# An mLSTM branch's output product as four pairs of seven block products, and an attention branch that adds to it

## The reference

```python
um  = h_m * silu(za);   y_m = um @ w_out_mlstm     # 1024x1024 @ 1024x1024
ua  = o_a * silu(zb);   y_a = ua @ w_out_attn      # 1024x512  @ 512x1024
merged = sigmoid(ga) * y_m + sigmoid(gb) * y_a
x = x + gate * (merged @ w_out)                    # 1024x1024 @ 1024x1024
return rms_norm(x, g_final)
```

## Time and profile before

| | |
|---|---|
| median of 3 runs | 1370.96 us (1369.63 to 1371.36) |
| the profiled execution | 1371.11 us |
| its span, first to last instruction | 1369.3 us |
| outside the span | 1.8 us |
| PE / DVE / ACT / POOL busy | 98% / 62% / 42% / 34% |

### The profile page before, as it was taken

One profiled execution on the slowest core, in us unless ns is written; L12 is line 12 of the kernel. 1 busy time (PEld: TensorE's weight loads), 2 busy tenths in 40 slices (PEclk: granted clock), 3 DMA queues, 4 the chain that ended last, 5 costly groups with the idle time before them and its releaser, 6 DMA issues.

```text
span 1369.3 us, 17469 instructions
## 1 busy us (share of the span) xinstructions
PE 1345.7 (98%) x6453; PEld 1126.9 (82%) x6453; DVE 855.3 (62%) x1472; ACT 580.1 (42%) x1016; POOL 463.0 (34%) x298
## 2 busy tenths in 40 slices
PE   8999999999999999999999999999999999999998
PEld 6888888888888888888898788889878887888886
DVE  7988766573745444535368757866875766434586
ACT  7663353343444344332545446354545534111122
POOL 0096555554545555543002200210120022222551
PEclk9999999999999999999999999999999999999999
DMA  8522323323234343337231841553172165453543
GB/s 316 196 82 95 132 99 123 123 93 115 101 123 139 123 143 134 139 112 228 73 83 48 231 93 32 161 148 94 48 227 67 33 241 205 128 187 140 173 138 108
DMA packets 65454, 180.52 MB, mean 132 GB/s; under 512 B 22001, under 2 KB 22129, under 8 KB 63318
## 3 DMA queue, kind: packets, MB, share of 16 engines
q1 hardware_dynamic: 61082, 166.64, 36.9%
q10 hardware_dynamic: 3168, 8.70, 1.9%
q0 software_dynamic: 1120, 4.06, 1.0%
HBM read 132.49 MB, written 46.89 MB: 131 GB/s over the span
## 4 chain that ended last, share of the span: by engine, by line
PE 87%; DVE 6%; ACT 3%; DMA 2%; issue 1%; SPq 0%; POOL 0%; ACTq 0%; DVEq 0%
PE banks L592 23%; PE banks L594 23%; PE banks L593 23%; PE banks L1265 4%; PE banks L1390 2%; PE banks L1400 2%; PE banks L1350 2%; PE banks L1356 2%; DMA wraw<-in_w_all 1%; PE banks L1339 1%; PE banks L1348 1%; PE banks L1409 1%; PE banks L584 1%; PE banks L556 1%; PE banks L1378 1%
## 5 line engine op out<-in xcount | busy, mean ns | idle before, releaser
L1248 POOL TENSOR_TENSOR wlo<-wraw,whi 128x1024 fp32r<-128x1024 f32 x28 | 72.1, 2575 | 436.5 <-ACT whi L1468 411.1
L718 POOL TENSOR_TENSOR wlo<-w_sum,whi 128x512 fp32r<-128x512 f32 x112 | 165.2, 1477 | 137.4 <-ACT whi L843 137.4
L592 PE MATMUL banks<-t_hi,whi 128*128 128x512 f32 x448 | 174.3, 389 | 0.0
L593 PE MATMUL banks<-t_lo,whi 128*128 128x512 f32 x448 | 174.3, 389 | 0.0
L594 PE MATMUL banks<-t_hi,wlo 128*128 128x512 f32 x448 | 174.3, 389 | 0.0
L989 DVE TENSOR_TENSOR c_sum<-c_sum,banks 128x512 f32<-128x512 f32 x196 | 134.4, 686 | 44.7 <-PE banks L594 30.6
L592 PE MATMUL banks<-h_hi,whi 128*128 128x512 f32 x416 | 162.0, 389 | 0.0
L594 PE MATMUL banks<-h_hi,wlo 128*128 128x512 f32 x416 | 161.9, 389 | 0.0
L593 PE MATMUL banks<-h_lo,whi 128*128 128x512 f32 x416 | 161.8, 389 | 0.0
L843 ACT ACTIVATE whi<-w_sum 128x512 fp32r<-128x512 f32 x112 | 70.5, 630 | 165.5 <-PE banks L594 100.7
L592 PE MATMUL banks<-whi,h_hi 128*128 128x512 f32 x256 | 100.2, 391 | 1.4 <-POOL wlo L1248 1.4
(11 more groups left out here) (374 smaller groups left out, 2904.8 us busy)
## 6 DMA issues: line engine op xcount, KB each, us to landing
wraw<-in_w_all SPq DMA_DIRECT2D x72, 512.0 KB, 4.3
raw<-in_w_all SPq DMA_DIRECT2D x28, 512.0 KB, 4.4
queries_keys<-fin SPq DMA_DIRECT2D x12, 1024.0 KB, 4.0
qa<-queries_keys SPq DMA_DIRECT2D x12, 768.0 KB, 13.7
s_wada<-in_w_ada_cols SPq DMA_DIRECT2D x16, 512.0 KB, 8.2
attn_values<-fin SPq DMA_DIRECT2D x6, 1024.0 KB, 4.0
tn<-attn_values SPq DMA_DIRECT2D x12, 512.0 KB, 10.1
sig_c<-merge_gates SPq DMA_DIRECT2D x6, 1024.0 KB, 6.4
```

Of the source, the lines that this page charges most:

```text
L592: t_.matmul(out, w_hi, x_hi, start=first, stop=False)
L593: t_.matmul(out, w_hi, x_lo, start=False, stop=False)
L718: nc.gpsimd.tensor_tensor(wlo4[:, o % 4, :], source(r, j), whi4[:, o % 4, :].bitcast(F32), subtract).then_inc(s_split, 1)
L1248: nc.gpsimd.tensor_tensor(to, wraw[:, q % 2, :], hi.bitcast(F32), ALU.subtract).then_inc(w_split, 1)
```

## The change

The mLSTM branch's product is made as `blocks` makes its products: four pairs of tiles (`BRANCH_PAIRS`), each of seven products of 12 matmuls, joined in SBUF (`umo`) and multiplied there by the first gate. The attention branch follows for all eight tiles; `merge_tile` now multiplies its half tile by the second gate and adds it to `umo`. Loads, splits, buffers and banks are put in a new order for it. `finish` is unchanged but for names and where it waits.

```diff
 def turn_stats(i):                         # mix, SP queue
+    if i == HEADS - 1:
+        gather_branch()     # um_d -> um_raw tiles 0-3; xc -> um_raw tiles 6, 7 (512 KB each)
-    for q in range(2):
+    for q in range(2) if i < HEADS - 1 else ():
         sp.wait_ge(um_done, i * 2 + q + 1)
         sp.dma_start(um_d[i, q], xc[:, q, :]).then_inc(um_out[q], 16)
     sp.wait_ge(stat_out, (i + 1) * 16 * sum(STATS))
     sp.dma_start(ct[:]..., stat_d...).then_inc(ct_in, 16)
+    for k in range(KH, KT - 2) if i == HEADS - 1 else ():
+        sp.dma_start(T["um_raw"][:, k, :], um_d[k // 2, k % 2]).then_inc(T["tile_in"][k], 16)
...
 def tensor(pe):                            # merge
     for p in range(PLAIN): ... first_pairs(p, j, h)
-    branch(um_at(0), 0, 0, KT, UM_BANKS)
...
-        branch(ua_at(m), m, KT, HEADS, UA_BANKS)
+    for r in BRANCH_PAIRS:
+        for j in ORDER:                    # 5, 1, 2, 4, 6, 7, 3
+            product(r, j)    # waits: bank, s_split, and for the first pair t_lo_done
+    for m in range(KT):
+        attn_branch(m)       # waits: bw_split m + 1; bank: merged(m - 4, ...) from m = 4
...
 def vector(dve):                           # merge
-    scale_two, join_two, join_third, gate_attn      (last head)
-    for k in range(KB): split_low(k)
-    for k in range(2): out_low(k)
+    branch_rows(range(KH)); dve.wait_ge(pv_kept, 12 * HEADS + 1)
+    difference(5, up_right, up_left[0])    # each difference and low: 128 x 2048
+    weigh_groups(HEADS - 1)
+    low(1, up_left[0])
+    branch_rows(range(KH, KT))
+    difference(6, low_right[0], bt_raw[5], 5)
+    low(5, bt_raw[5])
+    scale_two, join_two, join_third, gate_attn      (last head)
+    weight_sums(PAIRS)
+    difference(4, low_left[0], bt_raw[6], 6)
+    low(2, ...); low(4, ...); low(6, ...)
+    difference(7, low_right[0], up_right)
+    low(7, bt_raw[7]); low(3, low_right[0])
+    for r in BRANCH_PAIRS:
+        if r + 1 in BRANCH_PAIRS: weight_sums(r + 1)
+        else: for k in range(HEADS): attn_low(k)
+        join(r)
+        for j in range(2): gate(2 * (r - PAIRS) + j)     # umo[:, m] *= sa[m]
     for m in range(KT):
         merge_tile(m)
-        if m + 2 < KT: out_low(m + 2)
+        if m < len(WO_AT):                 # WO_AT = ((0, 1), (2, 3), (4, 5), (6,), (7,))
+            for e in WO_AT[m]: out_low(e)
...
 def scalar(act):                           # merge, last part
+    attn_weights_high(0)                   # waits for gprod, WITH_BRANCH - 3
+    for k in range(HEADS): attn_high(k)
+    attn_weights_high(1)
     for m in range(KT):
+        if m + 2 < KT: attn_weights_high(m + 2)    # waits for attn_branch(m)
+        act.wait_ge(merged_half, merged(m, 4))
+        if m == KT - 1: act.wait_ge(mg_out, 16 * KT)
+        act.dma_start(mg_d[m], umo[:, m, :]).then_inc(mg_out, 16)
+        if m < len(WO_AT): out_high of the same pieces
...
 def sync(sp):                              # merge, last part
+    load_gate_b(2); load_gate_b(3); load_attn_weights(3)
+    for k in range(4, 8): load_out(k)
+    sp.wait_ge(merged_half, KT)            # all eight gate(m) done
+    for k in range(2): load_out(k)
+    for m in range(2, KT):
+        if m + 2 < KT: load_attn_weights(m + 2)
+        if m == 2: sp.wait_ge(merged_half, merged(1, 4)); load_out(2); load_out(3)
+        if m + 2 < KT: load_gate_b(m + 2)  # from m + 2 = 4: waits for merged(m, 4)
```

More of the change, by code:

```diff
@@ L1623, in scalar @@
             z_sigmoid(ZA + 1)
-        group_exp(HEADS - 1)
+        T["shared"]["group_exp"] = group_exp
     def vector(dve):
@@ L1949, in sync @@
+        for b in range(2):
+            sp.wait_ge(sig_in[b], 48)
+        load_gate_b(2)
+        load_gate_b(3)
+        load_attn_weights(3)
+        for k in range(4, 8):
+            load_out(k)
+        sp.wait_ge(merged_half, KT)
         for k in range(2):
             load_out(k)
-        for m in range(KT):
[L1952 to L1965, removed]
+        for m in range(2, KT):
+            if m + 2 < KT:
+                load_attn_weights(m + 2)
+            if m == 2:
+                sp.wait_ge(merged_half, merged(1, 4))
+                for k in (2, 3):
+                    load_out(k)
+            if m + 2 < KT:
+                load_gate_b(m + 2)
@@ L2081, in vector, with branch_rows, difference, low @@
         step = T["shared"]["step"]
-        def split_low(k):
+        def branch_rows(ks):
+            for k in ks:
+                dve.wait_ge(tile_in[k], 32)
+        def difference(j, x, y, first=None):
+            if first is not None:
+                dve.wait_ge(t_raw, raw_count(first))
+            v.tensor_tensor(bt_raw[j], x, y, ALU.subtract).then_inc(t_raw, 1)
+        def low(j, raw_):
+            hi, lo = factors[j]
+            dve.wait_ge(t_hi_done, high_count(j))
+            v.tensor_tensor(lo, raw_, f(hi), ALU.subtract).then_inc(t_lo_done, 1)
@@ new lines, in plus, with join @@
+        def plus(r, name, out, x, j):
+            dve.wait_ge(gprod, 1 + at_product(r, j))
+            dve.wait_ge(part_added, added_part(r, name) - 1)
+            v.tensor_tensor(out, x, bank(r, j), ALU.add).then_inc(part_added, 1)
+        def join(r):
+            c11, c12, c21, c22 = (umo[:, 2 * (r - PAIRS) + j, part] for j in range(2) for part in (LEFT, RIGHT))
+            dve.wait_ge(first_kept, r + 1)
+            plus(r, "u2", c21, c11, 6)
+            plus(r, "u4", c12, c21, 5)
+            plus(r, "c11", c11, c11, 2)
+            plus(r, "c22", c22, c12, 7)
+            plus(r, "v", c21, c21, 7)
+            plus(r, "c21", c21, c21, 4)
+            plus(r, "c12", c12, c12, 3)
@@ new lines, in merge_tile @@
+                dve.wait_ge(merged_half, merged(m, 2 * h + 1))
+                v.tensor_tensor(umo[:, m, tok], umo[:, m, tok], sb[m][:, tok], ALU.add).then_inc(merged_half, 1)
+        dve.sem_inc(T["added"], 4)
+        branch_rows(range(KH))
+        dve.wait_ge(pv_kept, 12 * HEADS + 1)
+        difference(5, up_right, up_left[0])
+        T["shared"]["weigh_groups"](HEADS - 1)
+        low(1, up_left[0])
+        branch_rows(range(KH, KT))
+        difference(6, low_right[0], bt_raw[5], 5)
@@ new lines, in vector @@
+        low(5, bt_raw[5])
+        for part in ("scale_two", "join_two", "join_third", "gate_attn"):
+            T["shared"][part](HEADS - 1)
+        dve.wait_ge(T["ua_done"], 2 * HEADS + 1)
+        weight_sums(PAIRS)
+        difference(4, low_left[0], bt_raw[6], 6)
+        low(2, low_left[0])
+        low(4, bt_raw[4])
+        low(6, bt_raw[6])
+        difference(7, low_right[0], up_right)
+        low(7, bt_raw[7])
+        low(3, low_right[0])
+        for r in BRANCH_PAIRS:
+            if r + 1 in BRANCH_PAIRS:
+                weight_sums(r + 1)
+            else:
+                for k in range(HEADS):
+                    attn_low(k)
+            join(r)
+            for j in range(2):
+                gate(2 * (r - PAIRS) + j)
@@ L2338 @@
     pairs += [[np.arange(c, c + P) for c in (DH * i, DH * i + P)] for i in range(1, HEADS)]
+    w_um = x["w_out_mlstm"][0]
+    for p in range(KT // 2):
+        for c in range(2):
+            w_all[PAIRS0 + 2 * (PAIRS + p) + c] = tiles(w_um[:, (2 * p + c) * P:(2 * p + c + 1) * P])
     for r, two in enumerate(pairs):
```

421 lines of the change are left out of this document (273 added, 148 removed).

## The result

| | before | after |
|---|---|---|
| median of the runs | 1371.16 us (1369.63 to 1371.76, 4 runs) | 1388.07 us (1382.53 to 1388.73, 4 runs) |
| profiled execution, its span | 1371.11, 1369.3 us | 1388.73, 1386.9 us |
| ratio, 95% interval | | 1.0116 (1.0089 to 1.0143) |

The change makes the kernel slower by 1.2%, 16.9 us. The forecast was slower by 4.7 (1375.7, range 1369 to 1383): the right side, and too small by 12.4.

The account below looks back on a forecast made before the run. The prediction took the changed stage to be bound by PE, with everything else just hidden. Its terms, -12.3 + 0.9 + 4.0 + 2.5 + 7.6 + 2.0, summed to +4.7 us: 1375.7 us, range 1369 to 1383.

Parts of the forecast that it names:

- the gain: mLSTM branch: 48 matmuls fewer (10.9 us) and the 1.4 us of waits at old splits gone; -12.3 us.
- Before the first product: Fifth of `first_pairs`: late `ct` delays DVE, ACT's queue and POOL's split; 0.9 us, within 0 and 3.
- The first pair of products: First branch pair: DVE and POOL take turns at the shared port, so PE waits; 4.0 us, bounds 0 and 6.
- The attention stage: Attention tile 5: weights queued behind a gate load that waits for tile 2 come late; 2.5 us, bounds 0.3 and 4.
- The start of `finish`: Tile 6's store, reload and split outlast tile 7's 24 attention matmuls, so PE runs dry; 7.6 us, 7 to 9.5.
- The clock: PE's clock falls during the wait at `finish` and must come back; 2.0 us, between 0 and 5.4.
- DMA becomes the bound in the attention stage: Rival: loads land 3 us later each, weights cost 5 to 8 us more, POOL's reload 2; 1384 us, chance 0.12.
- PE is never starved but once: Rival: only the start of `finish` and some clock remain; -3.5 us, 1367.5 us, chance 0.12.
- the gain and the new waits cancel: Rival: stalls ahead of `finish` of 3 to 5 us instead of 7.4; 1370 to 1373 us, chance 0.22.

Follow-up runs that it names:

- h1_rows_first: Changed kernel with POOL's reload issued only once tile 7 is wholly merged, so behind the row loads; 1390.57 us, ratio 1.0136.
- h2_reload_first: Changed kernel with POOL's reload as late as in h1_rows_first, but SP's row loads and ACT's x loads wait until it has landed; 1385.80 us.
- b2_weights_first: Changed kernel with SP issuing the weights of attention tile m + 1 ahead of the gate load of tile m; 1386.52 us, ratio 1.0112.
- a1_late_rows: Changed kernel with SP's three row loads and ACT's x loads waiting until POOL's reload has landed; 1385.07 us, ratio 1.0100.
- h3_after_look: The changed kernel unaltered, profiled once more; one run, 1390.37 us.
- h4_after_look: The changed kernel unaltered, one more profile; one run, 1387.53 us.
- a3_filler: Changed kernel with 60 matmuls of unused results on PE ahead of its wait for the split at `finish`; 1386.52 us, ratio 1.0110.
- b3_all_three: Changed kernel with the first token blocks split straight from `umo` in SBUF, softmax statistics first and attention weights first together; 1372.20 us, ratio 1.0010.
- b1_stats_first: Changed kernel with SP loading `ct` ahead of `um`, and ACT and DVE doing the statistics work first; 1383.48 us, ratio 1.0098.
- g1_all_five: b4_no_dram plus tiles 0 to 5 split before tile 6 is merged, and ACT's weight copy ahead of its difference copy; 1370.07 us, ratio 0.9986.
- d1_small_splits: Changed kernel with POOL's splits for the first pair's last five products doing 16 of 512 columns; 1381.99 us, ratio 1.0078.
- b4_no_dram: b3_all_three with every token block split from `umo` and no stores of merged tiles or reloads; 1371.15 us, ratio 1.0001.

## Why the prediction was too low

| term, as the prediction named it | forecast | measured |
|---|---|---|
| the gain | -12.3 | -12.3: 10.9 by the count of matmuls, and no row is left of the 1.4 at the old splits |
| Before the first product | 0.9 | 2.71 |
| The first pair of products | 4.0 | 1.51 |
| The attention stage | 2.5 | 3.61 |
| The start of `finish` | 7.6 | 14.34 |
| The clock | 2.0 | 5.2 |
| not foreseen: restarts and small slips | 0 | 2.5 (the rest) |
| sum | 4.7 | 17.6 |

**The step that failed is the start of `finish`.** Its chain was right link by link: tile 6 merged, store, reload, split. Two links were longer than the rows of before. The reload took 9.42 us instead of 4.65, because the row loads now go out ahead of it. The forecast took both durations from a place where nothing else was being moved, and wrote the press of other loads down as a bound of 1.9 us ("upward if the gates' loads press on the small packets", 9.5); it measured 4.8, and the loads that press are not the gates' but the rows of `finish`, which the forecast didn't name. The release of the row loads hangs on PE's last product (`BRANCH_DONE`), and the change moves just that: before, it came 4.68 us behind the reload, now it is within 1 us of it. That was to be read from the code. `h1_rows_first` and `h2_reload_first` show that the order is the cause. The other link is the store of tile 6: 5.1 to 5.4 us from tile 6 merged to POOL's issue in all four profiles of the changed kernel, 3.0 before, and 3.0 to 3.9 in the seven altered kernels in which POOL's issue waits for nothing later than this store. With 3.7 or less the reload comes ahead of the rows, with 5.1 behind them, so in the profiles this link decides the race (`b2_weights_first` loses it at 3.9, since its rows go out earlier). Why it varies was not found. The faster executions of the changed kernel (1382.1 to 1384.0 us) may be those that win the race; none of them was profiled, so that isn't shown.

**What else spreads the times.** `a1_late_rows` can't lose the race, and its times still spread over about 5 us. Two things in the profiles account for a part. In nine of the 18 the clock falls between 28 and 30 us, in `setup`, far ahead of the changed code and whatever the edit, and PE is 1.4 us later from there on (its 200th matmul behind the first starts at 42.65 instead of 41.28). Here `h3_after_look` and then the first profile of the same kernel:

```profile
29.00:30.00 1.00, 1.00 (x5) 0.95 (x4) 1.00 (x1) 0.97 (x1) 0.00 (x0) 0.50 0.94 356
...
29.00:30.00 1.00, 1.00 (x8) 0.86 (x7) 1.00 (x1) 0.97 (x2) 0.00 (x0) 1.00 0.99 369
```

And the first pair comes out in several ways: 1.1 to 1.5 us of waits in eight profiles, 2.3 to 2.4 in five (`h4_after_look`, unaltered, among them), and one wait of 3.8, with a fall of the clock behind it, in `b2_weights_first` and `h2_reload_first`. In those two POOL's first split of the pair began just ahead of DVE's difference (1138.74 and 1138.80 in `h2_reload_first`; 1141.13 and 1139.47 in the changed kernel). That this order is the cause was not tested.

**The clock was mis-sized too.** One fall was foreseen, three came. The one at `finish` cost 98.2 - 95.8 = 2.4 us (`a3_filler`), against the 2.0 taken. The other two are had by comparing with `b3_all_three`, where the clock stayed up: from PE's return at the fifth of `first_pairs` to the first branch product 23.53 us after (1122.13 to 1145.66) and 21.93 there (1122.18 to 1144.11), so 1.6; and from tile 5's return to the end of the stage, 72 matmuls in both, 18.65 and 17.38, so 1.3. By the rule of the Trainium skill that the prediction weighed (TensorE: Matmul & The Clock Gate, section "HAM oscillation — how this bites in real kernels"), each wait that is long enough is paid again in the next stretch; these three agree with it.

**Before the first product** was within its bounds, and the chain was the one named: `ct` late, ACT's queue behind it, POOL's split behind that. It was priced too low. The split began at 1119.61, 4.0 us later than before, where 2.4 was reckoned. With `ct` early the wait falls from 2.7 to 1.45 (`b1_stats_first`); with the weight copy also ahead of the copy of 128x2048 (1.92 us) in ACT's queue it is 0.16 (`g1_all_five`).

**The first pair** has the mechanism given, DVE and POOL in turns: without POOL's work there is no wait (`d1_small_splits`). DVE's last `low` was forecast to end at 1162.3 and ended at 1159.75 + 2.77 = 1162.52, but that is luck. The forecast counted 6.5 us of POOL's work in full and no wait of DVE for ACT, which it left at "can add 2 us". By the rows the seven operations took 20.1 us instead of 16.1, so POOL held them up by 4, and DVE waited 3.1 us for ACT: two errors that cancel. The term cost less, 1.51 instead of 4.0, because PE came to it 3.5 us later than reckoned (1145.66, not 1142.2): the wait at the start and its clock had been paid before. The terms were added as if each stood alone. The Trainium skill (SBUF — State Buffer, section "Who interferes with whom") says that the port pair is held exclusively; the pairs of 3.38 and 3.34 us agree.

**The attention stage** was right in cause and nearly in size. The weights of tile 5 are queued right behind the gate load that waits for tile 2:

```profile
1247.82 0.33 SPq L1997 DMA_DIRECT2D gate<-merge_gates  x1
1248.19 0.43 SPq L1984 DMA_DIRECT2D wraw<-in_w_all  x1
...
1253.69 0.63 ACT L2173 ACTIVATE whi<-wraw 128x512 fp32r<-128x512 f32 x1 [3.44 <-DMA wraw<-in_w_all]
```

SP issued that gate load 23.4 us after PE began the stage (1224.41), where 22 was reckoned, and ACT's copy starts 5.5 us after the weights' issue, where 2.7 was reckoned for their landing. `b2_weights_first` takes the wait down to 0.8.

**The rivals.** *DMA becomes the bound in the attention stage* (1384) gave the nearest time, from the wrong place: it put 5 to 8 us on weights and 2 on the reload, and it was the reload that was hit, in `finish`. *PE is never starved but once* fell: there are four places. That *the gain and the new waits cancel* is what `b3_all_three` and `b4_no_dram` came to, by edits.

**Where the 12.3 us went.** No single wait eats them. Take away the DRAM way, the late statistics and the late weights, and the kernel stands level with the one before; two more edits give 0.14%. Each time the next wait comes up: behind the one at tile 5 the one at `finish`, behind that the one for `gf`.

## What to carry to other kernels

When a change shortens the bound engine's work, list every transfer whose release hangs on that engine's progress, and compare its new issue time with the critical transfer's: a lead of a microsecond decided 5 us here. A duration read where the queues are empty is a lower bound where they are not. Waits in a row are not independent: reckon each from when PE arrives there by the terms before it, and put a chance of the clock's price on the short waits too, not only on the longest one: here it fell after waits of 2 to 3 us in some executions and not in others.

## What the runs showed of the hardware

- The clock fell after short waits, and late. After a wait of 2.71 us PE was back at 1122.13, at a clock of 0.93 in 1122 to 1123, then 0.50, which is 1.2 GHz, to 1126, as the windows above show. After the 3.61 us before 1255.71 likewise. Yet `b3_all_three` waited 2.70 us at the start of `finish` and its clock stayed at 1.00, which is 2.4 GHz, through the 6 us that followed; `b4_no_dram` waited 2.67 us at the same place and its clock fell; and `g1_all_five`, after its wait of 2.00 us, shows 0.50 in 1150 to 1153. The length of a wait alone doesn't tell. Of `b3_all_three`, and then of `b4_no_dram`:

```profile
1272.00:1274.00 2.00, 0.95 (x4) 0.84 (x5) 2.00 (x2) 0.00 (x0) 1.51 (x3) 1.00 0.88 262
1274.00:1280.00 6.00, 5.88 (x24) 4.24 (x24) 1.07 (x2) 0.00 (x0) 5.49 (x6) 1.00 0.95 334
...
1270.00:1272.00 2.00, 2.00 (x6) 1.56 (x5) 0.00 (x0) 0.00 (x0) 2.00 (x2) 0.50 1.05 342
```

- A wait of PE costs about 0.25 us more than the row says. Matmuls of a split trio start 0.68 us from trio to trio; across the wait of 0.96 us at 1160.47 it is 1160.47 - 1158.67 = 1.80, 1.12 more, and the trio behind it took 0.77, 0.09 more: 1.21 in all. In `b3_all_three` the product with the wait of 1.25 us takes 4.25 us from start to start, against 2.72.
- An operation's size doesn't set its time when the port is held: in `d1_small_splits` POOL's splits of 16 columns still lasted 1.3 to 2.3 us each:

```profile
1152.31 2.26 POOL L2047 TENSOR_TENSOR wlo<-num,whi 128x16 fp32r<-128x16 f32 x1
```
